# One chunk of the last pair's gates moves between the last pair's tiles; y comes back in two token parts; last steps go to the score banks

## The reference, cut to what matters

```python
q, k, v, g = _split_a(u @ w_in)            # block A; block B splits in four equal parts
...                                        # attention: o, [tokens, 1024]
y = (o * jax.nn.silu(g)) @ w_out
h = layer_norm_2(DEEPNORM_ALPHA * h + gate[:, None, :] * y, ln_g[i], ln_b[i])
```

## Time and profile before

| | us |
|---|---|
| median of three runs (2068.91 to 2070.28) | 2069.14 |
| the profiled execution, its own time | 2074.76 |
| its span, first to last instruction | 2072.9 |
| PE busy | 1998.6 |
| DVE, ACT, POOL busy | 1077.8, 832.3, 822.3 |

### The profile page before, as it was taken

How to read it: one execution, slowest core, us unless ns; L and a number is a source line. 1 busy time by engine, 2 the same in 40 slices (tenths; PEclk the granted TensorE clock), 3 DMA queues, 4 the chain that set the end, 5 groups by cost and what they waited for, 6 DMA issues and landing times.

```text
span 2072.9 us, 36871 instructions
## 1 busy us (share of the span) xinstructions
PE 1998.6 (96%) x14882; PEld 1657.1 (80%) x14882; DVE 1077.8 (52%) x2223; ACT 832.3 (40%) x1636; POOL 822.3 (40%) x586
## 2 busy tenths in 40 slices
PE   7999999999999899999999899999999999999896
PEld 6888888888887788888888788778888888888774
DVE  5566467667754555556666623724434334334526
ACT  4100100100137366556666510744555555555401
POOL 3433333423456523212212435545435445445446
PEclk9999999999999999999999899999999999999898
DMA  4322322322232310100000323221111111112143
GB/s 158 132 101 92 111 82 92 112 92 82 81 102 83 113 34 22 34 34 34 35 22 24 132 95 110 77 92 46 47 52 52 47 46 51 51 42 87 47 142 122
DMA packets 48471, 156.01 MB, mean 75 GB/s; under 512 B 5296, under 2 KB 8240, under 8 KB 48176
## 3 DMA queue, kind: packets, MB, share of 16 engines
q1 hardware_dynamic: 47296, 152.40, 21.6%
q10 hardware_dynamic: 1008, 1.27, 0.2%
HBM read 132.94 MB, written 20.71 MB: 74 GB/s over the span
## 4 chain that ended last, share of the span: by engine, by line
PE 64%; POOL 3%; DVE 3%; issue 2%; ACT 1%; DMA 1%; DVEq 0%; SPq 0%; POOLq 0%
PE psum L851 15%; PE psum L853 14%; PE psum L852 14%; PE psum L1034 8%; PE psum L986 7%; PE psum L1002 5%; DMA w_raw<-weights_in 1%; POOL act_buf L703 1%; POOL w_lo L691 1%; PE psum L860 1%; DVE logits L1703 1%; POOL rstd L714 1%; PE psum L1012 0%; ACT logits L1292 0%; POOL act_buf L701 0%
## 5 line engine op out<-in xcount | busy, mean ns | idle before, releaser
L851 PE MATMUL psum<-u_hi,w_hi 128*128 128x512 f32 (+1 forms) x1440 | 547.1, 380 | 14.8 <-POOL w_lo L691 7.7
L689 POOL CAST w_hi<-w_raw 128x1024 fp32r<-128x1024 f32 x140 | 156.6, 1119 | 949.9 <-DMA w_raw<-weights_in 949.9
L852 PE MATMUL psum<-u_lo,w_hi 128*128 128x512 f32 (+1 forms) x1440 | 528.2, 367 | 0.0
L853 PE MATMUL psum<-u_hi,w_lo 128*128 128x512 f32 (+1 forms) x1440 | 528.1, 367 | 0.0
L691 POOL TENSOR_TENSOR w_lo<-w_raw,w_hi 128x1024 fp32r<-128x1024 f32 x140 | 350.7, 2505 | 11.2
L851 PEld LDWEIGHTS psum<-u_hi,w_hi 128*128 128x128 f32 x1440 | 274.3, 190 | 69.1 <-issue 16.3
L853 PEld LDWEIGHTS psum<-u_hi,w_lo 128*128 128x128 f32 x1440 | 274.7, 191 | 45.4
L852 PEld LDWEIGHTS psum<-u_lo,w_hi 128*128 128x128 f32 x1440 | 274.7, 191 | 39.2
L1292 ACT ACTIVATE logits<-logits,neg_max 128x640 f32<-128x640 f32 (+2 forms) x288 | 226.6, 787 | 82.3 <-DVE neg_max L1703 81.2
L1314 ACT ACTIVATE prob_t<-psum 128x320 f32<-128x320 f32 (+1 forms) x288 | 119.1, 414 | 265.3 <-PE psum L1002 265.2
L1301 ACT ACTIVATE logits<-logits,row_rec 128x640 f32<-128x640 f32 (+1 forms) x288 | 218.5, 773 | 0.0
(11 more groups left out here) (157 smaller groups left out, 3005.3 us busy)
## 6 DMA issues: line engine op xcount, KB each, us to landing
w_raw<-weights_in SPq DMA_DIRECT2D x140, 512.0 KB, 3.5
w_ada<-w_ada_in SPq DMA_DIRECT2D x48, 512.0 KB, 3.4
residual<-act_buf SPq DMA_DIRECT2D x4, 2048.0 KB, 7.6
tab<-bias_tab_in SPq DMA_DIRECT2D x16, 496.5 KB
res<-residual SPq DMA_DIRECT2D x26, 256.0 KB, 3.5
act_buf<-x_t_in SPq DMA_DIRECT2D x8, 512.0 KB, 13.5
staged<-a_y SPq DMA_DIRECT2D x6, 640.0 KB, 2.9
y_all<-staged SPq DMA_DIRECT2D x6, 640.0 KB, 10.9
```

The lines of the kernel that those rows point to most:

```text
L689: pool.tensor_copy(w_hi[:, slot, :], w_raw[:, slot, :]).then_inc(w_hi_done, 1)
L851: pe.matmul(out, wh, xh, start=first, stop=False)
L852: pe.matmul(out, wh, xl, start=False, stop=False)
L853: return pe.matmul(out, wl, xh, start=False, stop=last)
```

## The change

1. The gate chunk of pair 7 over latent tokens 512 to 1023 is made last in its stage (in layer 0 it was the second of three), is left out of the parts of pair 6, and is projected in tiles 0, 1 and 2 of pair 7 (3, 3 and 2 steps).
2. y is loaded for tokens 0 to 511 (layer 0 also context) when all but that chunk are done, and for tokens 512 to 1023 after it; casts and low halves are split likewise, with `split_late` on POOL and `low_late` on DVE. The third output weight unit is loaded and split between the two.
3. In layer 1 the early chunks are ordered by tokens, and of the second two tile 6 has 4 steps (7 before) and tile 7 has 10 (7 before).
4. The "r" steps go to banks 0 to 3, two ahead of the third chunks' last step and two behind; the weight slots that they free are counted by `last_done`.
5. In layer 1 the layer norm rows are loaded behind the first two `res` loads, not ahead of them.

```diff
@@ out_chunks
-    row = [("p", o, n, o, 0, KT - 1) for o in range(2) for n in early] + [("o", 2, n, 2, 0, KT) for n in first]
-    row += [("r", o, n, o, KT - 1, 1) for o in range(2) for n in early] + [("o", 2, 1, 2, 0, KT)]
+    order = [(o, n) for o in range(2) for n in early] if layer == 0 else [(o, n) for n in early for o in range(2)]
+    row = [("p", o, n, o, 0, KT - 1) for o, n in order] + [("o", 2, n, 2, 0, KT) for n in first]
+    row += [("o", 2, 1, 2, 0, KT)]
@@ early_parts
-    parts = [[], [], [], [(a0, 0, 3), (a1, 0, 3)], [(a0, 3, 5), (a1, 3, 5)], [(a0, 5, 7), (a1, 5, 7)]]
-    return parts + ([[(b0, 0, 5)], [(b0, 5, 7), (b1, 0, 7)], [(third, 0, 4)], [(third, 4, 7)]], [[(b0, 0, 7)], [(b1, 0, 7)]])[layer]
+    late = STAGES[layer][-1][-1]
+    parts = [[(late, 0, 3)], [(late, 3, 6)], [(late, 6, 8)]]
+    parts += [[(a0, 0, 3), (a1, 0, 3)], [(a0, 3, 5), (a1, 3, 5)], [(a0, 5, 7), (a1, 5, 7)]]
+    return parts + ([[(b0, 0, 5)], [(b0, 5, 7), (b1, 0, 7)], [(third, 0, 4)], [(third, 4, 7)]],
+                    [[(b0, 0, 4)], [(b0, 4, 7), (b1, 0, 7)]])[layer]
...
+Y_FIRST = (((0, HALF), (S, C)), ((0, HALF),))
@@ sync
+            if layer == 1:
+                sp.wait_ge(gated, TILE0[1] + PAIRS * TILES[1])
+                for dst, src in ((g_row, "ln_g3"), (b_row, "ln_b3")):
+                    sp.dma_start(...).then_inc(rows_loaded, 16)
...
-        load_y(0)
+        load_y(0, y_loaded, Y_FIRST[0], AO_CHUNK - 1)
         load_early(0)
+        load_unit(AO_UNIT + 2)
+        load_y(0, y_more, LAT_CHUNKS[1:], AO_CHUNK)
@@ gpsimd
+        def split_late(layer, *pairs):
+            for k in pairs:
+                if k < STAGED:
+                    pool.wait_ge(y_more[k], 16 * (layer + 1))
+                else:
+                    pool.wait_ge(pj_done, (AO_CHUNK, BO_CHUNK)[layer])
+                src = y_all[:, k, HALF:S] if k < STAGED else y_buf[layer][k % 2][:, HALF:S]
+                pool.tensor_copy(u_hi[:, k, HALF:S], src).then_inc(y_late_hi, 1)
...
             else:
                 split_y(1, 5, 6)
+                split_late(1, 0, 1, 2, 3)
             bias_tile(j, 5)
+            if not more:
+                split_late(1, 4, 5, 6)
+                split(BO_UNIT + 2)
             if more:
                 split(n + 2 + W_SLOTS)
                 first_bias(j + 1)
-                split(n + 3 + W_SLOTS)
+                if j + 2 < PAIRS:
+                    split(n + 3 + W_SLOTS)
@@ tensor
+        def last_step(layer, c):
+            last_pair_there(layer, c)
+            consumed(pe, next(e for e in EARLY[layer] if (e.pair, e.n) == (c.pair, c.n)))
+            slot, w = c.unit % W_SLOTS, slice(c.k0 * P, (c.k0 + 1) * P)
+            product(bank(c.index % 4)[:, 0:c.tn], ..., True, True).then_inc(last_done, 1)
...
+            for c in LAST[layer][:2]:
+                last_step(layer, c)
             for c in third:
                 last_pair_there(layer, c)
                 work(layer, [(c, KT - 1, KT)])
+            for c in LAST[layer][2:]:
+                last_step(layer, c)
@@ vector
+        def low_late(layer, k):
+            dve.wait_ge(y_late_hi, (KT - 1) * layer + k + 1)
+            src = y_all[:, k, HALF:S] if k < STAGED else y_buf[layer][k % 2][:, HALF:S]
+            dve.tensor_tensor(u_lo[:, k, HALF:S], src, u_hi[:, k, HALF:S].bitcast(F32), ALU.subtract).then_inc(y_late, 1)
...
+                    late = ({5: (0,), 6: (1, 2), 7: (3, 4), 8: (5, 6)}, {5: (0, 1, 2, 3), 6: (4, 5, 6)})[layer]
+                    for k in late.get(t, ()):
+                        low_late(layer, k)
```

More of the change, by code:

```diff
@@ L126, in lay_out @@
             row.sort(key=lambda c: STARTS[layer].index((c.kind, c.n)))
+        row.sort(key=lambda c: (c.kind, c.pair, c.n) == ("g", PAIRS - 1, 1))
         stages.append([c._replace(index=index + n) for n, c in enumerate(row)])
@@ L141, in out_chunks, with last_steps @@
     return [Chunk(index + i, kind, o, n, unit + u, *ALL_CHUNKS[n], k0, steps) for i, (kind, o, n, u, k0, steps) in enumerate(row)]
+def last_steps(layer):
+    return [c._replace(index=4 * layer + i, kind="r", k0=KT - 1, steps=1) for i, c in enumerate(sorted(EARLY[layer], key=lambda c: c.pair))]
 A_CHUNK = GROUPS * L1_CHUNKS
@@ L151 @@
 EARLY = tuple([c for c in row if c.kind == "p"] for row in OUTS)
+LAST = tuple(last_steps(layer) for layer in range(2))
+LAST_END = {c.unit: c.index + 1 for row in LAST for c in row}
 AGAIN = tuple(row[-len(again):] for row, again in zip(OUTS, OUT_AGAIN))
@@ L447, in build @@
     y_stored, y_loaded = sem("y_stored"), [sem(f"y_loaded{k}") for k in range(STAGED)]
+    y_more, y_late_hi, y_late = [sem(f"y_more{k}") for k in range(STAGED)], sem("y_late_hi"), sem("y_late")
     y_hi_done, y_split, y_split_pool = sem("y_hi_done"), sem("y_split"), sem("y_split_pool")
@@ L583, in store_y, with load_y @@
             sp.dma_start(staged[layer][pair], buf[:, :]).then_inc(y_stored, 16)
-        def load_y(layer):
-            sp.wait_ge(pj_done, (AO_CHUNK, BO_CHUNK)[layer])
+        def load_y(layer, loaded, spans, chunks):
+            sp.wait_ge(pj_done, chunks)
             sp.wait_ge(y_stored, 16 * STAGED * (layer + 1))
             for k in range(STAGED):
-                sp.dma_start(y_all[:, k, 0:(TC, S)[layer]], staged[layer][k]).then_inc(y_loaded[k], 16)
+                for t0, tn in spans:
+                    sp.dma_start(y_all[:, k, t0:t0 + tn], staged[layer][k, :, t0:t0 + tn]).then_inc(loaded[k], 16)
         def load_early(layer):
@@ L641, in _ @@
             for kind, pair in A_PLAN[j + 1]:
-                if kind != "t":
+                if kind != "t" and (kind, pair) != ("g", PAIRS - 1):
                     load_unit(CHUNKS[0][kind, pair][0].unit + W_SLOTS)
@@ L663, in _ @@
             load_unit(n + 2)
[L664 removed]
             if j < STAGED:
+                load_unit(n + 3)
                 store_y(1, j)
[L667 removed]
+        load_y(1, y_loaded, Y_FIRST[1], BO_CHUNK - 1)
         load_early(1)
[L669 to L671 removed]
+        load_unit(BO_UNIT + 2)
+        load_y(1, y_more, LAT_CHUNKS[1:], BO_CHUNK)
         load_out(1)
@@ L765, in _ @@
             pool.wait_ge(y_hi_done, k + 1)
-            pool.tensor_tensor(u_lo[:, k, :], y_all[:, k, :], u_hi[:, k, :].bitcast(F32), ALU.subtract).then_inc(y_split_pool, 1)
+            for t0, tn in Y_FIRST[0]:
+                ins = pool.tensor_tensor(u_lo[:, k, t0:t0 + tn], y_all[:, k, t0:t0 + tn], u_hi[:, k, t0:t0 + tn].bitcast(F32),
+                                         ALU.subtract)
+            ins.then_inc(y_split_pool, 1)
+        split(AO_UNIT + 2)
+        split_late(0, *range(KT - 1))
         pool.wait_ge(gated, TILE0[1])
@@ L1112, in attention @@
                     for part in PARTS[layer][pair][t]:
+                        if part[0].kind == "g":
+                            work(layer, [part])
+                            continue
+                        if part[0].n == 1:
+                            pe.wait_ge(y_late, (KT - 1) * layer + part[2])
+                            work(layer, [part])
+                            continue
                         below = [k for k in POOL_LOW[layer] if k < part[2]]
@@ L1831, in residual_sum @@
                 add = res[:, place, span]
+            g = ada[:, 24 * layer + 16 + o, c.n // 2:c.n // 2 + 1]
+            if c.kind == "r":
+                dve.wait_ge(last_done, c.index + 1)
+                dve.scalar_tensor_tensor(out, bank(c.index % 4)[:, 0:c.tn], g, add, ALU.mult, ALU.add)
+                return
             dve.wait_ge(pj_done, c.index + 1)
-            g = ada[:, 24 * layer + 16 + o, c.n // 2:c.n // 2 + 1]
             dve.scalar_tensor_tensor(out, pj[c.index % 2][:, 0:c.tn], g, add, ALU.mult, ALU.add).then_inc(pj_free[c.index % 2], 1)
@@ L1838, in output_sums @@
             dve.wait_ge(y_split, sum(LOW_COUNT[:layer + 1]))
-            for c in OUTS[layer][len(EARLY[layer]):-len(AGAIN[layer])]:
+            n = len(EARLY[layer])
+            third = OUTS[layer][n:n + (2, 1)[layer]]
+            for c in LAST[layer][:2] + third + LAST[layer][2:]:
+                residual_sum(layer, c)
+            for c in OUTS[layer][n + len(third):-len(AGAIN[layer])]:
                 residual_sum(layer, c)
```

30 lines of the change are left out of this document (21 added, 9 removed).

## The result

| us | before | after |
|---|---|---|
| median of the runs made together | 2069.24 (4 runs) | 2057.47 (4 runs, 2056.75 to 2059.64) |
| the profiled execution, own time | 2074.76 | 2057.81 |
| its span | 2072.9 | 2056.0 |
| PE busy | 1998.6 | 1986.9 |
| mean granted clock | 0.983 | 0.991 |

The ratio after to before is 0.9943, 95% interval 0.9931 to 0.9955: 11.8 us faster. Forecast were 26.3 faster and 2043; the time lies above the range of 2036 to 2056.

What follows compares the result with a forecast made beforehand. PE was taken as the bound, so time comes only from its holes, mainly in each layer's last pair. Gains of 15.4 (layer 0) and 10.9 (layer 1), together 26.3, off the median 2069.1 gave 2043 us; range 2036 to 2056.

Steps and rivals of the forecast that it cites:

- The bias stall of 3.1 in layer 1: End of pair 6: PE's outputs newly wait 3.1 us for POOL's bias and DVE's reduction, so pair 6 gains 2.4, not 5.5.
- The end: Last steps of each layer: four more banks gain 2.0 us in layer 0, earlier res loads 4.0 in layer 1.
- The wait of tile 6 for b_y: Layer 1, last pair: four late lows ahead of tile 5's gating make PE wait about 2 us; cost 2.3.
- the clock in layer 0 stays at 1.00: Layer 0, last pair: counted at full clock, with 0.95 or more from 1135 to 1165 as a sign of being right.
- the rivals: Four alternative outcomes: fourth tile late (chance 0.15), moved steps not hidden (0.08), no bias stall (0.10), clock stays down (0.05).
- the fourth tile stays late: Rival, chance 0.15: POOL's chain or loads miss tile 3, fourth iterations keep 13.04 and 12.89, 11.3 us less gain, 2054.
- 8.8 + 8 steps at 0.73 with their start = 14.6: Layer 0, last pair, tiles 0 to 2: work without waits at full clock plus the moved steps; 16.64 becomes 14.6 us.
- 6.8 for the fourth: Layer 0, last pair, fourth iteration: 6.8 us instead of 13.04, if POOL is done and the clock is up.
- the steps are the same in both, so I take the difference from the median: Whole kernel: the 26.3 us gain, worked out on a profiled execution 5.6 above the median, is subtracted from the median 2069.1.
- 0.5 for the late chunk's gate: Tile 3, last pair: 0.5 us added because ACT and DVE take that gate in tile 2 ahead of the gating.
- Pair 6, layer 0: Losing eight 512-token steps, worth 5.5 us, gains 5.3 (bounds 4 and 5.5).
- the four late lows: Layer 1, tile 5 of the last pair: DVE's lows ahead of its gating, 0.6 us each alone, 2.4 together; cost 2.3.

Runs made afterwards that it cites:

- e0: The kernel before, unchanged, profiled a second time: span 2065.5 us.
- e7: The kernel before, unchanged, profiled a third time: span 2068.9 us.
- e3: The kernel before with only the end's changes (last early steps in banks 0 to 3, layer norm rows behind the first two res loads): 2062.16 us, ratio 0.9966.
- the filled kernel: The kernel before with 9, 9 and 6 unused matmuls in tiles 0 to 2 of each layer's last pair, nothing moved: 2067.97 us, ratio 0.9991.
- bias first: The kernel after, with POOL building the first bias tiles of layer 1's last pair before splitting the weight unit: 2054.47 us, ratio 0.9929 to before.

## Why the prediction was wrong, step by step

**What held.** PE sets the time, and the holes are the three waits for row maxima a layer; the moved steps fit into them (0.4 and 0.3 left). The bias stall of 3.1 in layer 1, found from rows that nothing had named as a problem, came exactly, with its half clock. The end: 2.0 + 4.0 forecast, 7.0 measured alone. The wait of tile 6 for b_y: 2.3 forecast, 1.86 seen. That the clock in layer 0 stays at 1.00 through the stretch held as well. None of the rivals came true as told; the sum of 11 less that "the fourth tile stays late" gives comes near, but by another mechanism: POOL's lows and the loads were in time.

**The step that failed first** is the price of the holes: "8.8 + 8 steps at 0.73 with their start = 14.6" and 6.8 for the fourth, "the steps are the same in both, so I take the difference from the median". It sums against one execution in which PE lost more than usual: to the lower clock in layer 1, to the clock and a wait for POOL in layer 0. By the four traces with the old order of work (before, e0, e7, and e3 up to the end) the first four iterations take 27.3 in layer 0 and 30.3 in layer 1 in the mean, not 29.68 and 30.99. With 24.39 and 27.10 after, 2.9 and 3.2 are won on average where 8.3 and 6.0 were forecast. The first trace's own time was 5.6 above the median, and that was no constant ahead of the steps: of the 7.4 us between the first trace and e0, 5.1 sat in just the stretch to be improved and 1.5 behind the last outputs of layer 1, of which 1.1 in the stretch that the end's change shortens. For e7 against e0 it is otherwise: of 3.4 us, the first four iterations hold -1.8 in layer 0 and +3.05 in layer 1, 0.6 lies ahead of layer 0's last pair and 1.4 behind the last outputs.

**Tile 3** was mis-sized: "0.5 for the late chunk's gate, which ACT and DVE must now take in tile 2 ahead of the gating that PE's scores wait for". It measured 1.87 and 2.18. The chain in tile 2 is lows, take, gating, in layer 1:

```profile
1915.42 2.52 DVE L1811 TENSOR_TENSOR u_lo<-y_all,u_hi 128x512 fp32r<-128x512 f32 x2
1917.86 0.67 DVE L1745 SCALAR_TENSOR_TENSOR b_y<-b_y,psum 128x512 f32<-128x512 f32 x1
1918.46 0.28 DVE L1804 SCALAR_TENSOR_TENSOR b_y<-psum,b_y 128x128 f32<-128x128 f32 x1
```

Only the take was counted, at less than its 0.67, and the lows not at all, since they had stood there before. But there too PE's scores waited behind them in layer 1, and the sum for tile 3 carried no term for it:

```profile
1932.12 0.58 PE L986 MATMUL psum<-bk_hi,bq_hi 64*128 64x256 f32 x1 [1.24 <-DVE b_y L1734]
```

The rest had been hidden by PE's slow clock: PE at 1.2 GHz came for its scores later, in layer 0 later than DVE. The run without these lows shows their share, and the filled kernel has about the same wait in layer 1 (2.27) with nothing moved; in layer 0 it has 0.69. The fourth iterations came out 1.7 and 2.0 above the working, together 3.7 us.

**Pair 6, layer 0**: 3.35 for 5.3. Before had no idle time of PE there; after has 1.4, such as

```profile
1134.22 0.38 PE L1035 MATMUL psum<-ak_hi,aq_hi 64*128 64x256 f32 x1 [0.28 <-DVE a_y L1804]
```

That is the bound "an iteration could fall on the chain's floor"; the value taken was too near the full 5.5. The other 0.7 has no wait that I can name. Tiles 0 to 2 of layer 0 took 5.30 + 5.31 + 5.25 = 15.9 for the 14.6 worked out: with three steps in it PE's own work fills an iteration of 5.27 (3.05 + 2.2 by the prediction's prices), and the 5.0 of layer 1's first iteration, where there were none, was no measure of it.

**Tiles 5 to 7, layer 1**: the four late lows were priced right (2.48 for 2.4), with the two sums behind them, which stood ahead of this gating before as well,

```profile
1936.86 2.48 DVE L1818 TENSOR_TENSOR u_lo<-y_all,u_hi 128x512 fp32r<-128x512 f32 x4
1939.26 1.40 DVE L1918 SCALAR_TENSOR_TENSOR early<-psum,ada,early 128x512 f32<-128x512 f32 x2
```

but behind the wait of 1.86 the clock fell to 0.83, which wasn't counted:

```profile
1940.00:1950.00 10.00, 8.41 (x73) 6.86 (x74) 6.43 (x16) 4.44 (x9) 0.00 (x0) 0.83 0.24 79
```

and the last two iterations lost 3.68 instead of 2.3. The rule of the Trainium skill (SBUF — State Buffer, Who interferes with whom) by which these lows would cost 3.3 did not apply: POOL does nothing while they run. It applies in tile 2, where POOL's lows and splits run: in layer 0 a low takes 2.21 instead of 1.02, in layer 1 1.26 (2.52/2) instead of 0.62 (2.48/4), and there the prediction had no term for it.

**The size of it all.** In the traces 9.4 us are missing (26.3 forecast, 16.9 seen): 3.0 and 2.1 in the first four iterations, 2.0 and 0.7 up to them, 0.7 and 1.4 later in layer 1's pair; the end and the rest gave 0.5 more. The other 5.1 are the first trace against the medians. By the mean of the old-order traces the moved chunk's parts come to 3.4 + 1.7 us in pair 6 and 2.9 + 3.2 in the first four, less 3.7 later in layer 1's pair and 0.1 elsewhere: 7.4, where it gives 3.9 (2.1 to 5.8) when timed alone. Most of the gap is in which executions were traced. The one profiled of the moved chunk alone, 2064.41, is 1.4 under the median of its 11, and the three of the kernel before have a mean of 2070.9, 1.3 above the median of 2069.62; their difference of 6.5 less these two is 3.8. Which stretches make up the rest stays open: there is one trace of each changed kernel.

## What to carry to other kernels

Before a forecast rests on time lost at a low clock, take profiles of several executions: the loss is not a constant of the kernel, and what the holes cost in one trace is not what filling them brings. When PE gets faster in a stretch, everything that its slowness covered is late: add up, for each tile, what stands on DVE and ACT ahead of what PE waits for, what was already there too, at the length that it has beside POOL. And price the two halves of a change by themselves: here the small edit at the end brought more than the large one.

## What was not expected of the hardware

- The same wait of PE is followed by the 1.2 GHz level in one execution and not in another. In the kernel before, at the end of iteration 0 of layer 1's last pair, in e0 and then in e7:

```profile
1911.43 1.31 PE L1034 MATMUL psum<-prob_t,b_v 128*64 128x128 f32 x20 [1.95 <-DVE neg_max L1703]
```

```profile
1910.59 2.40 PE L1034 MATMUL psum<-prob_t,b_v 128*64 128x128 f32 x20 [1.96 <-DVE neg_max L1703]
```

- In the changed kernels it is alike: waits of 2.18 us with a window at 1.00 (after, tile 3), 2.19 at 0.83 (bias first, tile 3), 1.86 at 0.83 (after, tile 6).
- 21 executions of the kernel before have clocks of 0.983 to 0.988 and times of 2066.95 to 2072.74; those of the filled kernel have 0.990 to 0.992 and spread nearly as far, 2065.68 to 2069.50. The clock thus isn't all of the spread.
- DVE's low halves of 512 and 256 columns take 1.02 us with POOL idle and 2.21 beside POOL's subtractions, and there 2.18 as instructions that read one tensor.
